# Output projection 1 by weight rows with tokens on partitions, and post-norm, residual, pre-norm and the first two units of FFN 1 in two token halves

## The reference

```
merged = (gates[:, :, 0] * y_ml + gates[:, :, 1] * y_gla
          + gates[:, :, 2] * y_conf + gates[:, :, 3] * y_sc)
y = merged @ w_o                                  # output projection 1, 1024 x 1024
x = x + g_t * rms_norm(y, tm_post_g)              # post-norm and residual
h = rms_norm(x, cm_pre_g) * (1.0 + sc_c) + sh_c   # pre-norm of FFN 1
y = conv_ffn(h, ffn_w_up, ffn_dw_w, ffn_w_down)   # 3-tap convolution over tokens, silu(a) * v
x = x + g_c * rms_norm(y, cm_post_g)
```

## Time and profile before

| what | before |
|---|---|
| median of 3 runs | 1668.8 us (1668.79 to 1670.48) |
| the profiled execution | 1672.08 us, its span 1670.1 us |
| granted clock of TensorE, mean | 0.986 |
| busy: PE, PEld | 1616.4 us (97%), 1313.0 us (79%) |
| busy: DVE, ACT, POOL | 922.8 us (55%), 614.2 us (37%), 239.4 us (14%) |
| HBM | 165.54 MB read, 100 GB/s over the span |

### The profile page before, as it was taken

The page is one execution under the profiler, slowest core; times in us unless marked ns, Lnnn a source line. Parts: engine busy times, 40 slices in busy tenths (PEclk is TensorE's granted clock), DMA queues, the critical chain, the costliest instruction groups (busy, mean ns, idle before and its releaser), DMA issues.

```text
span 1670.1 us, 20144 instructions
## 1 busy us (share of the span) xinstructions
PE 1616.4 (97%) x7710; PEld 1313.0 (79%) x7710; DVE 922.8 (55%) x1275; ACT 614.2 (37%) x788; POOL 239.4 (14%) x132
## 2 busy tenths in 40 slices
PE   5999999989999799999999999999999999999998
PEld 5887678767888488888888887877788888888887
DVE  5559355437786744444432667766335656556333
ACT  4333353233234443333322532344543433333223
POOL 1210023220002011011000000343342111110000
PEclk9999999989999899999999999999999999999999
DMA  9233113205773123333222234222123333333221
GB/s 336 76 101 101 51 51 101 76 26 188 240 227 101 51 76 100 100 100 91 98 90 99 76 101 136 64 76 77 51 76 101 112 85 92 100 100 100 101 92 59
DMA packets 192228, 170.44 MB, mean 102 GB/s; under 512 B 9543, under 2 KB 180900, under 8 KB 192164
## 3 DMA queue, kind: packets, MB, share of 16 engines
q1 hardware_dynamic: 174240, 150.16, 29.0%
q10 hardware_dynamic: 16948, 16.89, 3.2%
q0 software_dynamic: 976, 2.52, 0.4%
...
HBM read 165.54 MB, written 2.10 MB: 100 GB/s over the span
## 4 chain that ended last, share of the span: by engine, by line
PE 90%; DVE 6%; ACT 2%; DMA 1%; issue 1%; SPq 0%; POOL 0%; DVEq 0%; ACTq 0%
PE bank L1283 22%; PE bank L1285 21%; PE bank L1284 21%; PE bank L1290 6%; PE bank L1292 6%; PE bank L1291 6%; DVE w_lo L1890 1%; DVE work L2028 1%; PE bank L1375 1%; PE bank L1833 1%; DMA work<-in_x 1%; PE bank L1597 1%; ACT w_hi L724 1%; PE bank L1387 1%; PE bank L1818 1%
## 5 line engine op out<-in xcount | busy, mean ns | idle before, releaser
L1283 PE MATMUL bank<-h_hi,w_hi 128*128 128x512 f32 (+1 forms) x1568 | 616.6, 393 | 8.2 <-DVE h_lo L1908 4.0
L1285 PE MATMUL bank<-h_hi,w_lo 128*128 128x512 f32 (+1 forms) x1568 | 607.1, 387 | 0.0
L1284 PE MATMUL bank<-h_lo,w_hi 128*128 128x512 f32 (+1 forms) x1568 | 606.2, 387 | 0.0
L1890 DVE TENSOR_TENSOR w_lo<-w_raw,w_hi 128x2048 fp32r<-128x2048 f32 x102 | 234.6, 2300 | 265.0 <-ACT w_hi L724 264.7
L1283 PEld LDWEIGHTS bank<-h_hi,w_hi 128*128 128x128 f32 x1568 | 296.4, 189 | 87.7 <-issue 22.9
L724 ACT ACTIVATE w_hi<-w_raw 128x2048 fp32r<-128x2048 f32 x131 | 250.1, 1909 | 280.2 <-PE bank L1292 171.1
L1285 PEld LDWEIGHTS bank<-h_hi,w_lo 128*128 128x128 f32 x1568 | 296.1, 189 | 60.6
L1284 PEld LDWEIGHTS bank<-h_lo,w_hi 128*128 128x128 f32 x1568 | 296.6, 189 | 58.1 <-issue 1.0
L638 POOL TENSOR_TENSOR w_lo<-w_raw,w_hi 128x2048 fp32r<-128x2048 f32 x29 | 134.3, 4632 | 546.8 <-ACT w_hi L724 546.8
L1290 PE MATMUL bank<-w_hi,y_hi 128*128 128x512 f32 x352 | 137.9, 392 | 0.9 <-DVE work L2378 0.9
L1292 PE MATMUL bank<-w_lo,y_hi 128*128 128x512 f32 x352 | 137.0, 389 | 0.0
...
## 6 DMA issues: line engine op xcount, KB each, us to landing
...
```

What stands on the lines that cost most here:

```text
L1283: pe.matmul(dst, w_hi[s][:, at:at + n], hi, start=first, stop=False, skip_group_check=onto)
L1284: pe.matmul(dst, w_hi[s][:, at:at + n], lo, start=False, stop=False, skip_group_check=onto)
L1285: return pe.matmul(dst, w_lo[s][:, at:at + n], hi, start=False, stop=last, skip_group_check=onto)
L1890: dve.tensor_tensor(w_lo[u % 2][:, :], raw[u % 2][:, :], w_hi[u % 2][:, :].bitcast(FP32), ALU.subtract)\
```

## The change

The projection's units are now 256 rows of w_o (all 1024 output channels for 2 of the 8 k). The product has tokens on partitions: tile c is token block c // 2 (128 tokens), column half c % 2. TensorE goes through units 0 and 1 for all tiles, then through units 2 and 3 for tiles 0 to 3, then for tiles 4 to 7. Behind tile 5 of unit 2 it turns the scaled rows of tokens 0 to 255, behind tile 5 of unit 3 it makes the mean square of the new x of these tokens. The factor of y is one number per row. x, its squares, the second factor and h are made in two halves of 256 tokens, and the first two up units go through half 0, then half 1, in matmuls of 256 columns; the second turn and the second mean stand between them. The second up unit's parts are put into `y_hi` and `y_lo`, ahead of the turn of its slot. Four ada columns units go behind the second mean, in a tile of their own.

The diff, cut to its core (helpers moved up from behind FFN 1 are left out, as are changed counts of semaphores):

```diff
-        take("wo", GEMM, 8)
-        take("ss1", HOLD)
+        for b in (7, 6, 5, 4, 0, 1, 2, 3):
+            take("wo", (b,))
+        for b in (7, 6, 5, 4):
+            take("res1", (b,))
         take("ss2", HOLD)
-        take("up1", GEMM, 4, FT // 2)
+        for b in (6, 0, 1, 6):
+            take("res1", (b,))
+        take("ss2", HOLD)
+        for b in (5, 4, 2, 3):
+            take("up1", (b,), 1, FT // 2)
+        take("ada2", (0,))
...
-            column_units("wo", A["w_o"][0], 0)
+            for k in range(4):
+                row_unit(U["wo"] + k, A["w_o"][0], k * 2 * P)
...
-            for u in range(U["wo"] + 2, U["up1"] + 1):
-                lo(u)
+            lo(U["wo"] + 2)
+            pool.wait_ge(sem("ahead_hi"), 1)
+            pool.tensor_tensor(y_lo[:, :, :].rearrange("p a b -> p (a b)"), raw[1][:, :],
+                               y_hi[:, :, :].rearrange("p a b -> p (a b)").bitcast(FP32), ALU.subtract).then_inc(parted[1], 1)
...
-            merged_hi(2)
-            for c in range(4):
-                split(U["wo"] + c + 1)
-                for n in (2 * c, 2 * c + 1):
-                    t = T["wo"][n]
-                    wait_full(act, t)
-                    if n == KT - 1:
-                        summed_square(n, bank[t.bank][:, :]).then_inc(sem("wo_squared"), 1)
-                        act.activation(ybuf[:, n, :], bank[t.bank][:, :], ACT.Copy).then_inc(read[t.bank], 1)
-                    else:
-                        act.activation(ybuf[:, n, :], bank[t.bank][:, :], ACT.Copy)
-                        summed_square(n, bank[t.bank][:, :]).then_inc(read[t.bank], 1)
-            split(U["up1"] + 1)
-            rsqrt(T["ss1"][0])
-            squares(1)
-            rsqrt(T["ss2"][0])
-            norm_hi(3 * KT)
...
+            def x1_square(b, cs):
+                for c in cs:
+                    act.wait_ge(sem("x_ready"), KT + KT * b + c + 2)
+                    act.activation(x1_sq[:, c:c + 2, half_of(b)], x[:, c:c + 2, half_of(b)], ACT.Square).then_inc(sem("x1_sq"), 1)
+
+            def half_rsqrt(b):
+                t, tok = T["ss2"][b], half_of(b)
+                wait_full(act, t)
+                ch.link(act.activation(rstd[:, tok], bank[t.bank][:, 0:HALF], ACT.Ln, bias=eps))
+                release(act.activation(rstd[:, tok], rstd[:, tok], ACT.Exp, scale=-0.5), t)
...
+            split(U["wo"] + 1)
+            merged_hi(2, range(4, KT))
+            for k in (1, 2):
+                split(U["wo"] + k + 1)
+            rows("wo", 0)
+            rows("wo", 1)
+            row_scaled("wo", 1)
+            act.wait_ge(w_used, U["y1"] + 1)
+            act.wait_ge(loaded[1], loaded_at(U["up1"] + 1))
+            act.activation(y_hi[:, :, :].rearrange("p a b -> p (a b)"), raw[1][:, :], ACT.Copy).then_inc(sem("ahead_hi"), 1)
+            x1_square(0, (0, 2, 4, 6))
+            split(U["up1"])
+            row_square("wo", 4)
+            row_square("wo", 5)
+            half_rsqrt(0)
+            row_factor("wo", 2)
+            act.nop().then_inc(hi_done, 1)
+            row_square("wo", 6)
+            ffn_hi(0, (0,))
+            row_square("wo", 7)
+            ffn_hi(0, (1,))
+            row_factor("wo", 3)
+            ffn_hi(0, (2,))
+            row_scaled("wo", 2)
+            ffn_hi(0, (3,))
+            row_scaled("wo", 3)
+            for c in (4, 6):
+                ffn_hi_of_pair(0, (c, c + 1))
+                x1_square(1, (c - 4,))
+            x1_square(1, (4, 6))
+            half_rsqrt(1)
+            ffn_hi(1, (0, 1))
+            ffn_hi_of_pair(1, (4,))
+            ffn_hi(1, (2,))
+            ffn_hi_of_pair(1, (5,))
+            ffn_hi(1, (3,))
+            ffn_hi(1, (6, 7))
...
+            def out_part(d, c):
+
+                u, t = U["wo"] + d, T["wo"][c]
+                tt, half = divmod(c, 2)
+                if d == 0:
+                    wait_free(pe, t)
+                for q in range(2):
+                    k = 2 * d + q
+                    pe.wait_ge(sem("h_ready"), hseen[0] + k + 1)
+                    mm = three_v(bank[t.bank][:, :], u, q * D + half * S, S, h_hi[:, k, tt * P:(tt + 1) * P], h_lo[:, k, tt * P:(tt + 1) * P],
+                                 k == 0, k == KT - 1)
+                if d == 3:
+                    done(mm, t)
+                return mm
...
+            def half_mean(b):
+
+                t, ks = T["ss2"][b], (range(2), (0, 1, 4, 5, 6, 7))[b]
+                pe.wait_ge(sem("x1_sum"), b + 1)
+                wait_free(pe, t)
+                for k in ks:
+                    if k >= 2:
+                        pe.wait_ge(sem("x1_sq"), 4 * b + k // 2 + 1)
+                    mm = pe.matmul(bank[t.bank][:, 0:HALF], const("ones_d"), x1_sq[:, k, half_of(b)], start=k == 0, stop=k == ks[-1])
+                mm.then_inc(sem("ss_done"), 1)
+
+            for d in range(2):
+                weights_ready(U["wo"] + d)
+                for c in range(KT):
+                    mm = out_part(d, c)
+                mm.then_inc(w_used, 1)
+            weights_ready(U["wo"] + 2)
+            for d, c in OUT_ORDER:
+                if (d, c) == (3, 0):
+                    weights_ready(U["wo"] + 3)
+                mm = out_part(d, c)
+                if (d, c) == (2, KT - 1):
+                    mm.then_inc(w_used, 1)
+                if (d, c) == TURN_BEHIND:
+                    rows_turned("wo", "res1", 0)
+                if (d, c) == MEAN_BEHIND:
+                    half_mean(0)
+            hseen[0] += KT
...
+                def up_part(b, m, ks):
+
+                    weights_ready(up + m)
+                    for k in ks:
+                        pe.wait_ge(sem("h_ready"), hseen[0] + KT * b + k + 1)
+                        for part in range(2):
+                            t = T["up1"][2 * m + part]
+                            if b == 0 and k == 0:
+                                wait_free(pe, t)
+                            hi, lo = (y_hi, y_lo) if m else (w_hi[up % 2], w_lo[up % 2])
+                            mm = three_of(bank[t.bank][:, half_of(b)], hi, lo, k * 256 + part * P, P, h_hi[:, k, half_of(b)], h_lo[:, k, half_of(b)],
+                                          b == 0 and k == 0, b == 1 and k == KT - 1, True)
+                            if b == 1 and k == KT - 1:
+                                done(mm, t)
...
+                    up_part(0, 0, range(4))
+                    rows_turned("wo", "res1", 1)
+                    up_part(0, 1, range(4))
+                    up_part(0, 0, range(4, KT))
+                    up_part(0, 1, range(4, 6))
+                    half_mean(1)
+                    for p in range(20, 24):
+                        ada_columns(T["ada2"][0], p, 20)
+                    up_part(0, 1, range(6, KT))
+                    for m in range(2):
+                        up_part(1, m, range(KT))
+                    hseen[0] += 2 * KT
...
-            gated("y1", last=True, low_at=U["wo"])
-
-            lo(U["wo"] + 1)
-            sums(22, 23)
-            ada_out(T["ada1"][0], 2 * KT, 4 * KT)
+            ada_out(T["ada1"][0], 2 * KT, 3 * KT)
             wait_read(dve, T["ada1"][0])
             ch.tick(dve.tensor_tensor(gain[:, 1, :], mod[:, 2 * KT:3 * KT], col("tm_post_g", 0, KT), ALU.mult))
             ch.tick(dve.scalar_tensor_tensor(out=gain[:, 2, :], in0=mod[:, 4 * KT:5 * KT], scalar=1.0, in1=col("cm_pre_g", 0, KT),
                                              op0=ALU.add, op1=ALU.mult))
-            ch.tick(dve.tensor_tensor(gain[:, 3, :], mod[:, 5 * KT:6 * KT], col("cm_post_g", 0, KT), ALU.mult))
-
             dve.wait_ge(ch.sem, ch.n)
+            gated("y1", last=True, low_at=U["wo"])
+
+            lo(U["wo"] + 1)
+            for c in (KT - 2, KT - 1):
+                merged_low(c)
+            sums(22, 23)
+            lo(U["wo"] + 3)
...
-            wait_read(dve, T["wo"][KT - 1])
-            residual("ss1", 1, ORDER[1])
-            lo(U["up1"] + 1)
-            norm_lo("ss2", gain[:, 2, :], 3 * KT)
...
+            def x_gained(res, k, b, c):
+
+                i, m = divmod(c, 2)
+                t = T[res][4 * b + i]
+                wait_full(dve, t)
+                dve.scalar_tensor_tensor(out=x[:, c, half_of(b)], in0=bank[t.bank][:, m * HALF:(m + 1) * HALF], scalar=gain[:, k, c:c + 1],
+                                         in1=x[:, c, half_of(b)], op0=ALU.mult, op1=ALU.add).then_inc(sem("x_ready"), 1)
+                if m:
+                    dve.wait_ge(sem("x_ready"), k * KT + KT * b + c + 1)
+                    dve.nop().then_inc(read[t.bank], 1)
+
+            def x1_sum(b):
+
+                last = (3, 1)[b]
+                for k in range(1, last + 1):
+                    dve.wait_ge(sem("x1_sq"), 4 * b + k + 1)
+                    if k > 1:
+                        dve.wait_ge(sem("x1_added"), k - 1)
```

(50 more changed lines are left out.)

256 lines of the change are left out of this document (119 added, 137 removed).

## The result

The changed kernel takes 1659.0 us (median of 4 runs, 1657.3 to 1659.9), the kernel before in the same session 1669.6 (4 runs): ratio 0.9931, 95% interval [0.9919, 0.9944]. The forecast was 1658.2. The profiled execution took 1659.94 against the 1672.1 that the sum was made against, so 12.1 less where 10.6 was forecast.

The account below looks back on a forecast made before the run. TensorE, busy for 97% of the span, bounds; only its waits or slow running can be won. Its terms from 505.11 sum to 587.0 against 597.64, 10.6 us less, taking 1668.8 to 1658.2; range 1654.8 to 1662.5.

Parts of the forecast that it names:

- the sum: Terms along TensorE from the projection's start to the second pair of up units: 587.0 against 597.64, 10.6 us less.
- the hole behind the projection: 21.7 us between output projection 1 and FFN 1's first matmul, holding none of TensorE's main work; it was to go.
- the whole walk: TensorE's path from the projection's first matmul to the second pair of up units: 92.5 us before, forecast at 81.9.
- The wait that the change brings in: TensorE waits 1.0 for the sum of squares of tokens 0 to 255, as POOL's low part holds VectorE's three adds.
- second rival: Weight loads are not hidden in FFN 1: 192 loads of 0.19 lie bare, 36.5 more, 1694.7; chance 0.02.
- first and third rival: Clock falls once in the new stretch, 1660.9, chance 0.10; clock stays low until iteration two, 1683, chance 0.04.
- The old cost: Low clock behind the hole: FFN 1's first 12 matmuls step at 0.43 where 0.23 is usual, 2.7 us.
- starts and waits: All other starts and waits in the stretch: 1.6 + 0.85 + 1.2 + 0.6 + 0.3, forecast at 4.55.
- 1.6 for 32 starts of a new k: In the first up units, the first matmul of each new k steps at 0.17, not 0.12; up to 1.6, counted whole.
- Ada columns: Late ada columns behind the second mean: 0.9, priced by eight records at 538.61 that took 0.95.
- that stretch: From TensorE's 505.11, the projection's start, to 597.64, the second pair of up units; outside it TensorE's order stays.
- fifth rival: The gain is given back, as FFN 1's loop or a late weight unit holds TensorE as long: 1668.8; chance 0.04.

Follow-up runs that it names:

- pool_halves: Changed kernel with POOL's low part of the second up unit made in two halves, the second behind the turned rows of tokens 256 to 511: 1658.6 us, ratio 0.9926.
- pool_late: Changed kernel with POOL making the whole low part of the second up unit only after the sum of squares of tokens 0 to 255: 1662.2 us, ratio 0.9946.
- mean_later: Changed kernel with the first mean of squares one tile later in the projection: 1659.2 us, ratio 0.9926.
- pairs_early: pool_halves plus ScalarE's first high part ahead of a square, and products of pieces 6 and 7 of h ahead of the second half's x updates: 1657.3 us, ratio 0.9922.
- same_again: The changed kernel run again, unedited: 1659.5 us, ratio 0.9932 to the kernel before.

## Why the prediction was right

**What bounds.** Right: the hole behind the projection was the place, and it filled. 81.35 against 81.9 for the whole walk. The step to trust in it was taking prices from the same operation elsewhere in the trace: the transposes, the fp32 mean and the 256-column step behind FFN 1 all came back to 0.25 or better.

**The wait that the change brings in.** Right in size (1.0 forecast, 0.97 measured), place and cause, pool_halves and pool_late show. The x updates pass while the adds are held, as forecast. What the prediction did not say is that removing this wait by itself (mean_later) wins nothing.

**Weight loads.** The 0.12 steps hold: 170 of the 192 matmuls of 256 columns are followed after 0.11 to 0.13, the others stand beside a wait or at the start of a group, with 0.19 for each load. The second rival's rule, by which loads would lie bare (1694.7), is out; the measurement decides against it.

**The clock.** It stayed at 1.00, so the first and third rival fell. The old cost was 2.7 in the text for the matmuls behind the hole; they gave back 2.5 in the execution that the sum was made against and 1.4 in another. A further 1.05 of low clock lay inside the 21.7 of the hole, since the means were priced as they ran.

**Feeding.** 4.55 for starts and waits, measured 3.85. The 1.6 for 32 starts of a new k was the wrong part: where the next piece of h has long been there, the step stays 0.12, and only behind a wait, however short, is it 0.22 (555.03 to 555.26). The prediction had taken the row behind FFN 1, which is such a case, for the rule. It also had pieces 4 to 7 of h ready in time; TensorE waited 0.20 for 6 and 7, and 0.58 in pool_halves, and pairs_early shows that the stretch hangs on them.

**Ada columns.** 0.9 forecast, 1.70 measured: the change puts 16 of these matmuls in that place, and I priced them by the row of eight. This is the one term that failed by counting.

**Where I said nothing moves.** "Outside that stretch the order on TensorE stays as it was" is true of the order and missed the banks. Of the 11.9 us of span, 11.2 are the stretch and 1.15 a wait in the down units that new banks removed; 0.15 is left over behind, and the stretch begins 0.55 later (its start lies between 503.9 and 506.8 in these executions, so this can't be put down to the change). So the sum was 1.15 short for the banks and 0.55 short in the stretch. That the forecast came within 0.8 of the median all the same is in part luck: the 1668.8 from which it was taken is the median of three runs, and two of these were faster than any of the 54 that came with the experiments. These 54 runs of the kernel before have a median of 1671.1; eight of them, with a mean granted clock of 0.987, lie at 1668.9 to 1669.9, the others, at 0.984 to 0.986, at 1670.2 to 1672.5. From 1671.1 the sum would have given 1660.5, where the changed kernel had 1659.0 and 1659.5. The differences of the medians are 10.7 in the first session and 11.3 in that of same_again, and 12.1 in the pair of profiles. The fifth rival had looked for time given back in FFN 1; the loop gave some more.
